# Six weight slots instead of eight, and the buffers that the freed space pays for, in a two-network fp32 kernel

## The reference, cut to what matters

```
for layer in 0, 1:                      # first network
    mod = silu(c) @ mod_w[layer] + mod_b[layer]       # 6 vectors: shifts, scales, gates
    h = rms_norm(x) * (1 + sc1) + sh1
    mix = even_mixer(h)  (layer 0: gated conv of width 31, stick-breaking attention)
        | odd_mixer(h)   (layer 1: conv of width 4, gates r and i, a linear recurrence, gelu branch)
    x = x + g1 * mix
    x = x + g2 * moe(rms_norm(x) * (1 + sc2) + sh2)   # 16 experts, top 2 of one group
for layer in 0, 1:                      # second network
    x = x + 0.5 * swiglu(rms_norm(x)); x = x + mixer(x); x = x + 0.5 * swiglu(rms_norm(x))
return rms_norm(x)
```

## Time and profile before

| | |
|---|---|
| median of 3 runs | 2119.07 us (2116.72 to 2119.67) |
| the profiled execution | 2119.07 us |
| its span, first to last instruction | 2117.3 us |
| outside the span | 1.8 us |
| granted PE clock, mean | 0.955 |
| PE busy | 1966.4 us, 93% of the span |
| DMA to HBM and back | 457.34 MB, mean 216 GB/s |

### The profile page before, as it was taken

How to read it: one execution, slowest core, us unless ns; L and a number is a source line. 1 busy time by engine, 2 the same in 40 slices (tenths; PEclk the granted TensorE clock), 3 DMA queues, 4 the chain that set the end, 5 groups by cost and what they waited for, 6 DMA issues and landing times.

```text
span 2117.3 us, 28128 instructions
## 1 busy us (share of the span) xinstructions
PE 1966.4 (93%) x11557; PEld 1685.4 (80%) x11557; DVE 1430.4 (68%) x1851; ACT 1137.3 (54%) x1499; POOL 81.6 (4%) x84
## 2 busy tenths in 40 slices
PE   4984899999979799999979999989999999989998
PEld 2843688888768578888869998779999998778997
DVE  2686588888776588888866565746556555656555
ACT  3341477676657467676745445535444443645443
POOL 0000011000000010010000000000000000000000
PEclk8996899999989899999989999989999999979999
DMA  9573688888759568888855655325555555514551
GB/s 362 181 269 127 220 296 301 296 303 294 278 189 352 175 216 306 293 304 293 309 190 179 199 188 192 113 90 178 191 183 177 198 188 190 174 60 142 197 191 59
DMA packets 209329, 457.34 MB, mean 216 GB/s; under 512 B 8848, under 2 KB 20776, under 8 KB 209192
## 3 DMA queue, kind: packets, MB, share of 16 engines
q1 hardware_dynamic: 204800, 450.99, 62.3%
q10 hardware_dynamic: 4392, 4.44, 0.6%
HBM read 454.35 MB, written 1.05 MB: 215 GB/s over the span
## 4 chain that ended last, share of the span: by engine, by line
PE 87%; DVE 7%; ACT 3%; DMA 1%; issue 1%; POOL 0%; SPq 0%; ACTq 0%; DVEq 0%; POOLq 0%
PE bank L290 84%; PE bank L1907 2%; DVE arena L1205 2%; DVE rest L617 2%; DVE arena L1197 1%; DMA raw<-in_mod_w 1%; PE bank L2166 1%; DMA raw<-in_od_out_w 0%; ACT arena L726 0%; ACT round L600 0%; DVE xres L1197 0%; PE bank L2148 0%; DVE small L1815 0%; ACT arena L1094 0%; DVE catTl L1205 0%
## 5 line engine op out<-in xcount | busy, mean ns | idle before, releaser
L617 DVE TENSOR_TENSOR rest<-raw,round 128x1024 fp32r<-128x1024 f32 (+1 forms) x760 | 888.7, 1220 | 250.5 <-ACT round L600 250.5
L600 ACT ACTIVATE round<-raw 128x1024 fp32r<-128x1024 f32 (+1 forms) x760 | 758.8, 1050 | 381.1 <-PE bank L290 377.7
L290 PE MATMUL bank<-hTh,round 128*128 128x256 f32 x1600 | 450.4, 281 | 15.2 <-DVE hTl L1197 12.8
L290 PE MATMUL bank<-hTh,rest 128*128 128x256 f32 x1600 | 448.2, 280 | 0.0
L290 PE MATMUL bank<-hTl,round 128*128 128x256 f32 x1600 | 448.2, 280 | 0.0
L290 PEld LDWEIGHTS bank<-hTh,round 128*128 128x128 f32 x1600 | 303.5, 190 | 21.6 <-issue 19.2
L290 PEld LDWEIGHTS bank<-hTl,round 128*128 128x128 f32 x1600 | 304.6, 190 | 1.0 <-issue 0.2
L290 PEld LDWEIGHTS bank<-hTh,rest 128*128 128x128 f32 x1600 | 304.8, 190 | 0.0
L290 PE MATMUL bank<-round,hTh 128*128 128x512 f32 x464 | 186.6, 402 | 6.6 <-DVE hTl L1197 2.9
L290 PE MATMUL bank<-round,hTl 128*128 128x512 f32 x464 | 183.1, 395 | 0.0
L290 PE MATMUL bank<-rest,hTh 128*128 128x512 f32 x464 | 182.0, 392 | 0.0
(11 more groups left out here) (220 smaller groups left out, 2525.7 us busy)
## 6 DMA issues: line engine op xcount, KB each, us to landing
raw<-in_ex_w SPq DMA_DIRECT2D x192, 1024.0 KB, 5.5
raw<-in_mod_w SPq DMA_DIRECT2D x48, 1024.0 KB, 6.9
raw<-in_ffn_w_gate SPq DMA_DIRECT2D x44, 1024.0 KB, 5.0
raw<-in_ffn_w_up SPq DMA_DIRECT2D x44, 1024.0 KB, 5.0
raw<-in_ffn_w_down SPq DMA_DIRECT2D x44, 1024.0 KB, 4.8
raw<-in_w_in SPq DMA_DIRECT2D x20, 1024.0 KB, 5.0
raw<-in_ev_in_w SPq DMA_DIRECT2D x10, 1024.0 KB, 13.8
raw<-in_od_in_w SPq DMA_DIRECT2D x8, 1024.0 KB, 5.2
```

What stands on the lines that cost most here:

```text
L290: return e.matmul(o, l, r, start=start, stop=stop, skip_group_check=True)
L600: e.activation(hi[:, h], raw[:, h], ACT.Copy).then_inc(S("hi"), 1)
L617: e.tensor_tensor(lo[:, h], raw[:, h], hi[:, h].bitcast(F32), ALU.subtract).then_inc(S("lo"), 1)
```

## The change

`NSLOT` goes from 8 to 6. That frees 16 KB per partition. Half of it becomes a buffer `acc` of its own ([2, 1024] floats), half makes the arena larger (14336 floats). `tmps` is gone and its users write to `acc`; `xn`, `GT`, `gr` and `muf` move to the end of the arena; `lng`, `lnb`, `wsT`, `wsr` move from `gbc` to `acc`. In `odd()` the exp of ACT signals a semaphore of its own and the square waits for that. The branch for experts with more than 128 tokens uses `acc` and drops a wait. PE counts up a semaphore `scattered` after each scatter, for which nothing waits.

```diff
-NSLOT = 8
+NSLOT = 6
...
+        acc = sb("acc", 2, D)
...
-        arena = sb("arena", 12320)
+        arena = sb("arena", 14336)
...
-        GT = [over(f"GT{i}", 9216 + 256 * i, 2, 128) for i in range(3)]
-        gr = over("gr", 9984, 2, NE, 2)
+        GT = [over(f"GT{i}", 12288 + 256 * i, 2, 128) for i in range(3)]
+        gr = over("gr", 13568, 2, NE, 2)
...
-        xn, tmps, acc = region(4096, 2, D), region(6144, 2, D), region(0, 2, D)
+        xn = region(12288, 2, D)
...
-        muf = rows[:, :, :].rearrange("p a b -> p (a b)")
+        muf = region(13056, 512)
...
-        lng, lnb = gbc[:, 0, 0:512], gbc[:, 0, 512:1024]
-        wsT = gbc[:, 1, 0:512].rearrange("p (g t) -> p g t", g=4)
-        wsr = gbc[:, 1, 512:1024].rearrange("p (g t) -> p g t", g=4)
+        lng, lnb = acc[:, 0, 0:512], acc[:, 0, 512:1024]
+        wsT = acc[:, 1, 0:512].rearrange("p (g t) -> p g t", g=4)
+        wsr = acc[:, 1, 512:1024].rearrange("p (g t) -> p g t", g=4)
...
-                    own.did(e.activation(rr[:, h4, :], rr[:, h4, :], ACT.Exp))
-                    own.see()
+                    e.activation(rr[:, h4, :], rr[:, h4, :], ACT.Exp).then_inc(S("odd_a"), 1)
+                    e.wait_ge(S("odd_a"), h + 1)
...
-                        tmp = tmps[:, th, nh * 512:(nh + 1) * 512]
+                        tmp = acc[:, th, nh * 512:(nh + 1) * 512]
...
-                            o, x = region(9216 + 512 * (j % 2), 512), quarter(th, nh)
-                            if ex + j:
-                                e.wait_ge(S(f"late{l}_x"), 8 * ex + 2 * j)
+                            o, x = acc[:, th, nh * 512:(nh + 1) * 512], quarter(th, nh)
...
+                    if ex < NE - 1:
+                        ins.then_inc(S("scattered"), 1)
```

## The result

The changed kernel takes 2139.8 us (median of 4 runs, 2137.8 to 2143.2) against 2117.9 us for the kernel before on the same chip (4 runs, 2115.2 to 2119.7): a ratio of 1.0107, 95% interval 1.0089 to 1.0126. It is about 22 us slower; the forecast was 2122.9 us, with 2128.5 as the upper end.

What follows compares the result with a forecast made beforehand. The prediction took PE, busy 93% of the span, to bound the kernel. It added 3.0 us for the odd mixer and 0.8 for the clock, all else 0, to 2119.07: 2122.9 us, range 2118.5 to 2128.5.

Steps and rivals of the forecast that it cites:

- The other edits: Whole kernel: moved buffers, overflow branch and semaphores change no instruction's shape and no wait; term 0.
- The rival that priced longer experts: MoE: landings vary by more than the 3.1 us of cover in many experts, adding 28 us: 2147; chance 0.05.
- How much later the loads come: All 428 loads: each is issued when load i + 2 is now; MoE, second network and start cost 0.
- Even mixer's output: Loads 34 to 36: load 34 lands 4.4 us after its present rounding, PE begins as now; 0, at worst 1.1.
- Odd mixer, +3.0: Loads 150 to 171: ACT waits for load 154, PE stalls behind it, a present idle vanishes; +3.0 us.
- gates piece: Odd mixer, piece 157: its rounding moves behind the square, PE is 3.3 us late, a stall of 2.3.
- the four places: Odd mixer: new PE stalls of 2.3 at piece 157, 1.4 at load 158, 1.7 at 164, 1.8 at 167.
- Clock term, +0.8: Odd mixer: new PE stalls may lower the clock, bounds 0 and 1.5 us each; half of one taken, +0.8.
- Slower queue: Rival: 1 MB takes 2.9 us instead of 2.55, delaying even mixer and load 154: 2125; chance 0.10.

Runs made afterwards that it cites:

- after_shifted: The changed kernel with raw and round buffers moved up by an unused 128 B: 2118.3 us, ratio 1.0003.
- before_off_128: The kernel before, eight raw buffers, with raw and round buffers moved up by 128 B: 2142.5 us, ratio 1.013.
- depth_alone: The kernel before with 6 raw buffers instead of 8 and every buffer at its old address: 2117.1 us, ratio 1.0012.
- depth_and_place: The kernel before with 6 raw buffers, raw and round buffers at the addresses of the changed kernel: 2143.8 us, ratio 1.013.
- depth_7: The kernel before with 7 raw buffers instead of 8 and every buffer at its old address: 2115.8 us, ratio 0.9984.
- both_apart_64: The changed kernel with activations 64 B past a multiple of 256 B, raw and round buffers at one: 2140.8 us, ratio 1.0112.

## Why the prediction was wrong, point by point

**The step that failed** is "The other edits": "No row shows an effect of an address. Term 0 from both sides". The absence of a row was no reason for a zero. Two edits that I had counted as free, `acc` ahead of the raw buffers and the larger arena, move the operands of nearly every matmul, and the term measures 21.5 us here (2139.8 less the 2118.3 of after_shifted). The same move alone gives ratio 1.013, 27 us, with eight buffers (before_off_128) and takes 2117.1 to 2143.8 us with six (depth_alone, depth_and_place). In place of the step: PE's pace follows the distance of the two operands modulo 256 B. The text did name PE in the MoE as what would show it, and the prediction's own test, that it is wrong "if MoE experts take longer, or if the second network's stages move", is what happened. The rival that priced longer experts (2147) had the wrong mechanism, late landings: no rounding in the MoE of the changed kernel was released by a load. No rival had matmuls at a slower pace without a wait.

**How much later the loads come**: right. Cover in the MoE held at six buffers (2.4 us at the nearest load of the first layer in the changed kernel, where 3.1 was read) and is just used up at five. The FFNs kept about 11 us (10.9 at the nearest load of the changed kernel, after the first loads; 10.2 in depth_alone).

**Even mixer's output**, term 0: right, and in its mechanism. The stage took 99.6 us before, 99.9 in the changed kernel and 99.4 in depth_alone. In depth_alone, where all here comes 3.2 us late, ACT waits 4.35 us for load 34 (forecast 4.4) and PE starts after the same 3.09 us of idle as before:

```profile
161.11 2.00 ACT L601 ACTIVATE round<-raw 128x1024 fp32r<-128x1024 f32 x2 [4.35 <-DMA raw<-in_ev_out_w]
...
164.78 0.74 PE L290 MATMUL bank<-round,catTh 128*128 128x512 f32 x1 [3.09 <-DVE rest L618]
```

**Odd mixer, +3.0**: right in its mechanism; that the size comes out as well is partly luck. The clean comparison is depth_alone with the kernel before, for there nothing else differs: 98.6 against 96.3 us. PE in depth_alone, timeline:

```profile
666.12 0.39 PE L290 MATMUL bank<-catTh,round 128*128 128x256 f32 x1 [2.07 <-DVE rest L618]
...
690.14 0.50 PE L290 MATMUL bank<-round,catTh 128*128 128x512 f32 x1 [1.73 <-DVE rest L618]
```

Stall at the gates piece: 2.07 us, forecast 2.3. At load 164: 1.73, forecast 1.7. At load 158: none, forecast 1.4. At load 167: 0.40, forecast 1.8. `mod_sums(18)`: 0.90 in two waits, forecast 0.9. The idle of 3.96 and the slow clock behind it are gone, 5.7 us gained, forecast 5.4. So PE waited 4.2 us in the four places where 7.2 were forecast, and the next point made up for it. Which of the four stalls come isn't fixed by the depth: in depth_and_place, also with six buffers, PE waited 1.86 us at the gates piece, 1.47 at load 158 and 1.93 at load 167, and not at load 164. There is also a slip in the recorded sum: with the difference at 689.6 and PE's start at 688.8 - 5.75 = 683.05, PE is 6.6 late, and 6.6 less 4.7 is a stall of 1.9 at load 164, not 1.7. The term goes by the 6.6 and stays.

**Clock term, +0.8**: too small; each of two stalls cost about the upper bound of 1.5. Windows of the matmuls in depth_alone, the stall and what follows it: length, busy PE, busy weight loads, clock, DMA share, GB/s:

```profile
664.00:666.10 2.10, 0.05 (x4) 0.00 (x0) 1.00 0.95 345
666.10:670.70 4.60, 4.58 (x26) 4.59 (x27) 0.63 1.05 408
...
688.40:690.10 1.70, 0.01 (x1) 0.00 (x0) 1.00 1.05 398
690.10:697.50 7.40, 7.36 (x27) 5.93 (x27) 0.77 0.74 288
```

After a stall of 2.07 us the clock was 0.63 for 4.6 us, which costs 4.6 x 0.37 = 1.7. After the 1.73 it was 0.77 for 7.4 us, again 1.7; measured from use to use, the matmuls behind either stall lost 1.6. So both stalls near 2 us brought the whole 1.5, and the one of 0.40 none: 3.2 in place of 0.8. It is no rule: in depth_and_place PE worked on at full clock for 3.8 us behind the stall of 1.86, and the clock was low only behind the next one, of 1.47:

```profile
669.20:673.00 3.80, 3.77 (x32) 3.69 (x32) 1.00 1.05 402
...
674.40:678.60 4.20, 4.13 (x23) 4.13 (x24) 0.62 0.90 331
```

In depth_7 a stall of 0.96 us was followed by 4.2 us at 1.00. In sum, depth_alone less the kernel before, the steps from the use of load 151 to that of 171 are +1.2 (loads 152 on), +3.7 (gates piece), +3.3 (load 164), -5.7, +0.3: +2.8 us, forecast 3.8 with the clock. (From the use of 142 on it is the 2.3 above, since the loads up to 151 went 0.5 faster.)

**Slower queue**: not seen. Right behind the stall in depth_alone the queue moved 408 GB/s. The Trainium skill ("DMA: Bandwidth & Descriptors", Specifications) states about 358 GB/s for one core; the trace disagrees, as it did before the change.

Without the move, the forecast would have stood: 6 buffers at the old places measure 1.0012 (0.9993 to 1.0031), and 3.8 us are 1.0018. The interval holds 1 as well, so it is the trace and not the time that shows the mixer's loss.

**What stays open.** Why the distance sets the pace isn't shown; no view has a row for it. Nor is it shown what picks one of the two paces at 192 B: the kernel before and depth_alone differ in it in whole FFNs (188.2 against 185.0 us in the second), after waits that differ by tenths of a microsecond. The other edits (places of `xn`, `GT`, `muf`, the four views, the semaphores) were not run by themselves; depth_and_place without them (1.013) and the changed kernel with them (1.0107) have overlapping intervals, and the 4 us between their medians have no explanation here.

## What to carry to other kernels

A buffer that is added, dropped or resized moves all that is laid out behind it, and on a kernel bound by TensorE that is an edit of its own: write down the start of each matmul operand modulo 256 B before and after, and put back the distance with a small gap (32 words here). Which distance is best was measured for the two kinds of load here alone, and they don't agree: 192 B or a mixture for the gate loads, 0 for the down loads. Then measure a change of depth by holding every address fixed, or the two effects are read as one. A PE that is busy for longer with the same matmuls and no new waits is read from the intervals between starts, since the listed durations hide it.

## What the runs showed of the hardware that I had not expected

- The pace of back-to-back fp32 matmuls with 128 x 256 moving data ranged from 113 to 120 ns a matmul (5.44 to 5.76 us for 48), by the distance of weights and moving data (0, 64, 128 and 192 B were run); of those with 512 columns from 227 to 233 ns (5.44 to 5.60 us for 24).
- The same distance of 64 B with both operands 128 B further on gives the same paces to 0.01 us (both_apart_64, the changed kernel). Everything on a multiple of 256 B is the slowest place for one operand order (gate loads) and the fastest for the other (down loads).
- At 192 B one kernel runs at two steady paces, 5.44 and 5.65 us a load, each held over many loads and changed only at the borders between kinds of loads.
- A TensorE stall of 2.07 us was followed by 4.6 us at a mean granted clock of 0.63 (part of them at the lower of its two levels, 1.2 GHz), one of 1.73 us by 7.4 us at 0.77 (depth_alone); the one of 0.40 us cost only itself. One of 1.86 us (depth_and_place) was followed by 3.8 us at 1.00.
